# Token chunks of 512, 512 and 128 in place of three of 384 in the projections and the mixture of a hybrid encoder layer

## The chip, the core and the metric

The kernel runs on one core of a Trainium2 chip. The metric is the device time of one execution in microseconds (us). TensorE is called PE in the profile, its weight loads PEld; VectorE is DVE, ScalarE is ACT, GpSimd is POOL and SyncE is SP. A `q` behind a name (SPq) is the queue in which that engine issues its transfers.

## What is computed

One layer of a streaming encoder for 1024 prompt tokens (one sequence) and 128 sample tokens (8 sequences of 16), width 1024. What matters here is the first half of the layer:

```python
h = rmsnorm(x, norm1_g) * (1 + sc1) + sh1
q, k, v, cb, cc, cv, ga, gb = jnp.split(h @ w_in, IN_SPLITS, axis=-1)   # 6 x 512, then 2 x 1024 columns
att = prompt_attention(q, k, v, rel_bias)          # sample_attention for the sample tokens
u = cc * cv;  y = sum(conv_w[j] * u_pad[:, j:j + L] for j in range(3)) + conv_b;  conv_out = cb * y
mix = (jax.nn.sigmoid(ga) * (att @ w_pa) + jax.nn.sigmoid(gb) * (conv_out @ w_pb)) @ w_o
x = x + gt1 * mix
```

The second half is a router and a mixture of 32 experts, which the change doesn't touch.

## The kernel before

**Precision.** Every float32 product is made of three matmuls (`product`, lines 1562 to 1567). Weights and activations are split into a high part, rounded to the type fp32r by ACT, and a low part, the remainder, made by DVE; the three are high by high, high by low and low by high. In `chunk_of` and in the mixture the stationary operand of a matmul is a 128x128 tile of the weights (in `ring_r`), the moving operand is a run of token columns of the activations (`hTh`, `hTl`), and the result is a piece of a PSUM bank of 512 float32 columns.

**Tokens.** The 1152 tokens lie side by side, the 128 sample tokens last. They are cut in three chunks of 384 columns (`TOKCH`, line 41). The last chunk, columns 768 to 1151, holds 256 prompt tokens and the 128 sample tokens; where prompt and sample results go to different tiles, `parts` (line 69) cuts it in two, and its evacuation is two instructions.

**Projections.** A unit is a slice of 128 output columns of a weight matrix, a 128x1024 tile. `project` (line 1589) runs over 4 units and for each over the three chunks; a chunk of a unit is 8 products, 24 matmuls, into one of the banks 4 to 7 in turn. `group` makes PE wait, before it writes a bank, until the evacuation of the group four before it has been counted (`gev_qk`, `gev_conv`, `cu_done`). Five matrices go this way: Q, K, CC, CV and CB of the convolution. V and the output projection have the weights as the moving operand, 512 wide, and don't use the chunks. ACT evacuates Q, K and CC, DVE multiplies CV into it (line 1229), and CB into the convolution's result Y (line 1258). Between CV and CB, DVE computes the convolution itself, for all four tiles, before its first multiplication by CB.

**First unit.** The first two chunks of unit 0 of Q are computed inside the loop over the nine token tiles of the first norm, at its steps t = 7 and 8 (lines 1620 to 1624). Each waits until DVE has finished as many token tiles as it covers (`n1_lo`).

**Mixture.** 24 steps (line 1781): for each of the 8 output tiles f, the three chunks. A step is 24 products, 72 matmuls: gate A and gate B (8 products each) and the projections of attention and convolution (4 each), into four banks; the steps alternate between banks 0 to 3 and 4 to 7. ACT takes the two sigmoids, DVE two multiplications and the sum, POOL writes the result to DRAM (`mix_d`). PE may start step i when step i - 2 is done (`g_done`). The weights of tile f + 1 are brought in, and split by ACT and DVE, during step 0 of tile f.

**End of the mixture.** The last weights of the output projection need the ring's slots, and are issued by SP once all matmuls of the mixture are done (`g_ready`, line 426).

Of the kernel before, what the change touches and what calls it, by code (L numbers as in the profile page):

```python
# [5 lines left out]
ALU = mybir.AluOpType  # L6
# [7 lines left out]
P = 128  # L14
D = 1024
KT = D // P
NP_TOK, SEQS, DEC = 1024, 8, 16
NS_TOK = SEQS * DEC
T = NP_TOK + NS_TOK
# [17 lines left out]
OVF = (2 * T) // CAP - 1  # L37
NBLK = E + OVF
SEQROW = SEQS
TC = T // 3  # L40
TOKCH = [(0, TC), (TC, TC), (2 * TC, TC)]


class Link:
# [17 lines left out]
def wait(eng, sem, value):  # L62
# [1 line left out]
    if isinstance(value, int) and value <= 0:  # L64
        return
    eng.wait_ge(sem, value)


def parts(c0, cn):

    out = []
    if c0 < NP_TOK:
        out.append((c0, min(c0 + cn, NP_TOK) - c0, False))
    if c0 + cn > NP_TOK:
        start = max(c0, NP_TOK)
        out.append((start, c0 + cn - start, True))
    return out


def build(nc, x_prompt, x_sample, cache_attn_k, cache_attn_v, state_conv, c_prompt, c_sample,  # L80
# [4 lines left out]
    with ExitStack() as ctx:  # L85
# [4 lines left out]
        def at(name, shape, offset, dt=F32):  # L90
            return nc.alloc_sbuf_tensor_at(name, shape, dt, offset=base + int(offset))
# [68 lines left out]
        def A(kb):  # L160
            return ARENA + kb * KB
# [10 lines left out]
        kT = at("kT", [P, HP, NP_TOK], A(90))  # L172
        kTs = at("kTs", [P, HP, NS_TOK], A(106))
# [36 lines left out]
        U = at("U", [P, HP, NP_TOK + 2], A(90))  # L210
# [80 lines left out]

        ps = psum("ps", [P, 8, 512])

        def u_part(m, c0, t0, tn, sample, g):
            src = ps[:, 4 + g % 4, t0 - c0:t0 - c0 + tn]
            if sample:
                return Us[:, m, :, 2:], src.rearrange("p (q t) -> p q t", t=DEC)
            return U[:, m, 2 + t0:2 + t0 + tn], src

        def bank(b, n=1):  # L300
            return ps[:, b:b + n, :].rearrange("p b c -> p (b c)")
# [16 lines left out]
        s = {n: sem(n) for n in names}  # L318
# [15 lines left out]
        UQ, UK, UV, UCC, UCV, UCB = [4 * i for i in range(6)]  # L334
# [172 lines left out]
        def _(pool):  # L507
# [121 lines left out]
            for i in range(24):  # L629
                f, (c0, cn) = i // 3, TOKCH[i % 3]  # L630
                pool.wait_ge(s["g_done"], i + 1)
# [91 lines left out]
        def _(act):  # L723
# [56 lines left out]
            g = 0  # L780
            for what in range(2):
                for m in range(HP):
                    for c0, cn in TOKCH:
                        if c0 == 0:
                            weights_high_to(4 * what + m + 3)
                        act.wait_ge(s["gemm"], g + 1)
                        src = ps[:, 4 + g % 4, 0:cn]
                        if what == 0:
                            nc.scalar.mul(qT[:, m, c0:c0 + cn], src, HD ** -0.5).then_inc(s["gev_qk"], 1)
                        else:  # L790
                            for t0, tn, sample in parts(c0, cn):
                                dst = kTs[:, m, t0 - NP_TOK:t0 - NP_TOK + tn] if sample else kT[:, m, t0:t0 + tn]
                                nc.scalar.copy(dst, src[:, t0 - c0:t0 - c0 + tn]).then_inc(s["gev_qk"], 1)
                        g += 1
            weights_high_to(UV + 4)
            for i in range(5):
# [59 lines left out]
            for m in range(HP):  # L856
                weights_high_to(UCC + m + 2)
                for c0, cn in TOKCH:
                    act.wait_ge(s["gemm"], g + 1)
                    for t0, tn, sample in parts(c0, cn):  # L860
                        nc.scalar.copy(*u_part(m, c0, t0, tn, sample, g)).then_inc(s["gev_conv"], 1)
                    g += 1


# [4 lines left out]
                weights_high_to(UCV + m + 3)  # L869
            g += 12 + 2  # L870
            act.wait_ge(s["conv_last"], 1)
            act.wait_ge(s["cu_done"], 17)

            nc.scalar.copy(atth[:], qT[:]).then_inc(s["b_hi"], 1)
            for m in range(HP):
                act.wait_ge(s["gemm"], g + 3 * m + 1)
                weights_high_to(UCB + m + 3)
                act.wait_ge(s["cu_done"], 16 + 3 * (m + 1))
                nc.scalar.copy(Yh[:, m, :], Y[:, m, :]).then_inc(s["b_hi"], 1)

            def mixture_high(t):
# [6 lines left out]
            for i in range(24):  # L888
                cn = TOKCH[i % 3][1]
                if i % 3 == 0:  # L890
# [104 lines left out]
            with act.If(n_ov > 0):  # L995
                with act.Fori(0, OVF) as o:
                    with act.If(o < n_ov):
# [10 lines left out]
                        dst = y_d.rearrange("(p b) d -> p b d", b=NBLK)[:, bass.ds(o + E, 1), :]  # L1008
# [31 lines left out]
        def _(dve):  # L1040
            link = Link(dve, s["link_dve"])
            V = nc.vector
# [23 lines left out]
            n = P - 1 + BAND - 4 * P  # L1066
# [149 lines left out]
            g = 12 + 12 + 5 + NT  # L1216
# [5 lines left out]
            for m in range(HP):  # L1222
                weights_rest_to(UCV + m + 3)
                for n, (c0, cn) in enumerate(TOKCH):
                    dve.wait_ge(s["gemm"], g + 1)
                    for t0, tn, sample in parts(c0, cn):
                        dve.wait_ge(s["gev_conv"], 4 * m + n + 1 + sample)
                        dst, src = u_part(m, c0, t0, tn, sample, g)
                        V.tensor_tensor(dst, dst, src, ALU.mult).then_inc(s["cu_done"], 1)
                    g += 1  # L1230
            dve.wait_ge(s["cu_done"], 16)
            dve.wait_ge(s["gemm"], g + 1)
            V.tensor_copy(Us[:, :, :, 0:2],
                          ps[:, 4 + g % 4, 0:HP * 16].rearrange("p (m q j) -> p m q j", m=HP, j=2)
# [20 lines left out]
            for m in range(HP):  # L1255
                for c0, cn in TOKCH:
                    dve.wait_ge(s["gemm"], g + 1)
# [276 lines left out]
        def _(pe):  # L1534
# [3 lines left out]
            n = SEQS + 1  # L1538
# [47 lines left out]
                                   hTh[:, k, c0:c0 + cn], hTl[:, k, c0:c0 + cn], k == 0, k == KT - 1)  # L1586
                last.then_inc(s["gemm"], 1)

            def project(u0, owner, base_count, split=False):

                done = 0
                for m in range(4):
                    for c, (c0, cn) in enumerate(TOKCH):
                        done += len(parts(c0, cn)) if split else 1
                        if u0 > 0 or m > 0 or c == len(TOKCH) - 1:
                            chunk_of(u0 + m, c, owner, base_count + done)
                        if c0 == 0:
                            release(u0 + m - 1)
                    used[1] = len(owners)
# [16 lines left out]
            for t in range(NT):  # L1616
                r = t % 2
                if 1 <= t < NADA - LEAD:
                    modulation(LEAD + t)
                if t >= NT - 2:  # L1620
                    c = t - (NT - 2)
                    pe.wait_ge(s["mod_sb"], NADA)
                    pe.wait_ge(s["n1_lo"], (c + 1) * TC // P)
                    chunk_of(UQ, c, "gev_qk", c + 1)
                pe.wait_ge(s["n1_h"], t + 1)
                wait(pe, s["n1_lo"], t - 1)
                for k in range(KT):
                    last = tr(bank(2 * r, 2)[:, k * P:(k + 1) * P], ht[:, r, k * P:(k + 1) * P], ident[:])
                last.then_inc(s["n1_tr"], 1)
            pe.wait_ge(s["n1_lo"], NT)  # L1630
            pe.wait_ge(s["mod_sb"], NADA)

            project(UQ, "gev_qk", 0)
            project(UK, "gev_qk", 12, True)
            pe.wait_ge(s["gev_qk"], 28)
            for i in range(5):
                b = group("gev_kout", i + 1)
                for m in range(HP):
                    src = kT[:, m, (4 + i) * P:(5 + i) * P] if i < 4 else kTs[:, m, :]
# [123 lines left out]
            pe.wait_ge(s["ks_at"], H * SEQS)  # L1763


            project(UCC, "gev_conv", 0, True)
            project(UCV, "cu_done", 0, True)
            pe.wait_ge(s["prev_in"], 16)
            b = group("gev_prev", 1)
            for m in range(HP):  # L1770
# [4 lines left out]
            for m in range(HP):  # L1775
                last = tr(ps[0:18, b, m * P:(m + 1) * P], lastu[:, m, :], ident[:])
            last.then_inc(s["gemm"], 1)
            project(UCB, "cu_done", 16)


            for i in range(24):
                f, (c0, cn) = i // 3, TOKCH[i % 3]
                if i == 1:
                    pe.wait_ge(s["cu_done"], 28)
                ua, ub, up = [slot_of(UGATE + 3 * f + j) for j in range(3)]
                wait(pe, s["g_done"], i - 1)
                b = 4 * (i % 2)
                for kind, (sl, un, k0, kn, xh, xl, br) in enumerate((
                        (ua, 0, 0, KT, hTh, hTl, 0), (up, 2, 0, 4, atth, attl, 1),
                        (ub, 1, 0, KT, hTh, hTl, 0), (up, 2, 4, 4, Yh, Yl, HP + 1))):  # L1790
                    if i % 3 == 0:
                        pe.wait_ge(s["w_lo"], UGATE + 3 * f + un + 1)
                        wait(pe, s["b_lo"], br)
                    for k in range(kn):
                        last = product(ps[:, b + kind, 0:cn], ring_r[:, sl, 0, k0 + k, :],
                                       ring_r[:, sl, 1, k0 + k, :], xh[:, k, c0:c0 + cn], xl[:, k, c0:c0 + cn],
                                       k == 0, k == kn - 1)
                    last.then_inc(s["g_ready"], 1)
                    if i == 0 and kind == 0:
                        release(UCB + 3)  # L1800
                    if i == 23 and kind in (1, 3):
                        pe.wait_ge(s["g_ready"], 4 * i + kind)
                        pe.sem_inc(s["unit_used"], 1)
                    if i % 3 == 0 and f > 0 and kind == 0:
                        pe.wait_ge(s["g_ready"], 4 * i)
                        pe.sem_inc(s["unit_used"], 3)
# [194 lines left out]
```

## Time and profile before

| | us |
|---|---|
| median of 3 runs | 1923.19 (1922.13 to 1927.28) |
| span of the profiled execution, from first to last instruction | 1918.4 |
| PE busy (matmuls) | 1676.0 (87%), 8467 matmuls |
| PE busy (weight loads) | 1388.9 (72%) |
| DVE busy | 962.2 (50%) |
| ACT busy | 766.2 (40%) |

The profile gives no total of its own for the profiled execution beside its span, which is 4.8 us shorter than the median of the runs. Busy time is the union of the durations of an engine's instructions. Matmuls are pipelined: a matmul is shown with a duration that reaches past the start of the next one, so the cost of one in a dense stream is read from start to start and not from its duration.

The first projections run until about 260 us, with an idle stretch of PE before 169 us; V and attention fill 260 to 570, the projections of the convolution 570 to 730, the mixture 730 to 1030, the output projection and the second norm 1030 to 1180. After that come routing and the experts.

### The profile page before, as it was taken

How to read it: one execution, taken by the hardware profiler on the slowest of the kernel's cores; microseconds unless marked ns; L12 is line 12 of the kernel's file. 1: busy time of each engine (PE TensorE's matmuls, PEld its weight loads, DVE VectorE, ACT ScalarE, POOL GpSimd, SP SyncE). 2: the span in 40 equal slices, each digit the busy share in tenths (PEclk: the TensorE clock that was granted, in tenths of full speed). 3: DMA queues.
4: the chain of work that ended last, by engine and by line, in shares of the span. 5: the costliest groups of instructions: out<-in, count | busy, mean ns of one | idle time of the engine just before them, and what ended most of it. 6: DMA issues, size and time to landing. Idle time of an engine off the chain costs nothing.

```text
span 1918.4 us, 22477 instructions
## 1 busy us (share of the span) xinstructions
PE 1676.0 (87%) x8467; PEld 1388.9 (72%) x8467; DVE 962.2 (50%) x1156; ACT 766.2 (40%) x869; POOL 216.4 (11%) x336
## 2 busy tenths in 40 slices
PE   6984999999989989999998994499999999999930
PEld 1244987886449989999997883377777777777720
DVE  0451102554320272222223545488888888888847
ACT  0221123663112022111121322077777777777734
POOL 2004401110000000000000002100000000000036
PEclk9997999999999999999998997699999999999965
DMA  9857512003421111211225333299999999999963
GB/s 344 284 84 219 191 64 71 1 2 113 157 68 54 44 34 31 83 50 50 58 71 199 121 99 110 92 398 398 396 396 395 395 394 394 396 391 393 342 220 142
DMA packets 194747, 371.34 MB, mean 194 GB/s; under 512 B 10699, under 2 KB 69107, under 8 KB 194546
## 3 DMA queue, kind: packets, MB, share of 16 engines
q1 hardware_dynamic: 170784, 289.92, 42.1%
q0 software_dynamic: 18976, 62.93, 10.2%
q10 hardware_dynamic: 4914, 17.49, 2.3%
q8 instruction: 51, 0.84, 0.2%
q14 instruction: 22, 0.18, 0.0%
HBM read 324.49 MB, written 47.89 MB: 194 GB/s over the span
## 4 chain that ended last, share of the span: by engine, by line
PE 74%; DVE 10%; ACT 6%; issue 3%; DMA 2%; another core or an unknown queue 2%; ACTq 1%; POOL 0%; SPq 0%; POOLq 0%; DVEq 0%; PEldq 0%
PE ps L1565 19%; PE ps L1567 18%; PE ps L1566 18%; PE ps L1548 4%; DVE mlo L1084 4%; ACT mhi L938 3%; PE ps L1692 3%; PE ps L1673 2%; ACT yy L958 2%; PE ps L1755 2%; PE ps L1732 2%; PE ps L1879 2%; PE ps L1682 1%; DMA bada<-in_b_ada_dram 1%
## 5 line engine op out<-in xcount | busy, mean ns | idle before, releaser
L1084 DVE TENSOR_TENSOR mlo<-mraw,mhi 128x2048 fp32r<-128x2048 f32 x188 | 420.5, 2288 | 38.9 <-ACT mhi L938 38.7
L938 ACT CAST mhi<-mraw 128x2048 fp32r<-128x2048 f32 x192 | 357.2, 1910 | 27.3 <-DMA mraw<-in_w_e_down_dram 27.2
L1565 PE MATMUL ps<-hTh,ring_r 128*128 128x384 f32 x864 | 291.2, 337 | 39.5 <-DVE ring_r L1084 31.6
L1567 PE MATMUL ps<-hTh,ring_r 128*128 128x384 f32 x864 | 290.6, 336 | 0.0
L1566 PE MATMUL ps<-hTl,ring_r 128*128 128x384 f32 x864 | 290.6, 336 | 0.0
L1565 PE MATMUL ps<-mhi,xTh 128*128 128x512 f32 x512 | 207.5, 405 | 22.0 <-DVE mlo L1084 19.6
L1566 PE MATMUL ps<-mlo,xTh 128*128 128x512 f32 x512 | 201.7, 394 | 0.0
L1567 PE MATMUL ps<-mhi,xTl 128*128 128x512 f32 x512 | 201.5, 394 | 0.0
L1565 PEld LDWEIGHTS ps<-hTh,ring_r 128*128 128x128 f32 x864 | 163.8, 190 | 41.2 <-DVE ring_r L1084 29.8
L1084 DVE TENSOR_TENSOR ring_r<-ring_f,ring_r 128x1024 fp32r<-128x1024 f32 x56 | 68.2, 1224 | 199.9 <-ACT ring_r L748 199.5
L1567 PEld LDWEIGHTS ps<-hTh,ring_r 128*128 128x128 f32 x864 | 163.6, 189 | 0.0
L1566 PEld LDWEIGHTS ps<-hTl,ring_r 128*128 128x128 f32 x864 | 163.5, 189 | 0.0
L1565 PEld LDWEIGHTS ps<-mhi,xTh 128*128 128x128 f32 x512 | 97.3, 190 | 53.9 <-DVE mlo L1084 28.5
L1567 PEld LDWEIGHTS ps<-mhi,xTl 128*128 128x128 f32 x512 | 97.1, 190 | 21.1
L1566 PEld LDWEIGHTS ps<-mlo,xTh 128*128 128x128 f32 x512 | 97.3, 190 | 18.6
L1565 PE MATMUL ps<-mhi,hhTh 128*128 128x512 f32 x256 | 103.3, 404 | 6.3 <-DVE mlo L1084 6.3
L1567 PE MATMUL ps<-mhi,hhTl 128*128 128x512 f32 x256 | 100.9, 394 | 0.0
L1566 PE MATMUL ps<-mlo,hhTh 128*128 128x512 f32 x256 | 100.7, 393 | 0.0
L748 ACT CAST ring_r<-ring_f 128x1024 fp32r<-128x1024 f32 x56 | 58.5, 1051 | 105.1 <-DMA ring_f<-in_w_in_dram 45.9
L1548 PE MATMUL ps<-aring,cT 128*9 128x512 f32 x192 | 87.7, 611 | 8.0 <-DMA bada<-in_b_ada_dram 8.0
L943 ACT CAST xTh<-ps 128x1024 fp32r<-128x1024 f32 x32 | 32.5, 1016 | 114.9 <-PE ps L1879 114.9
L1130 DVE CUSTOM_DVE_ANT_0 S<-ps,bias 128x640 f32<-128x640 f32 (+4 forms) x64 | 42.1, 657 | 63.3 <-PE ps L1674 63.2
(302 smaller groups left out, 2549.4 us busy)
## 6 DMA issues: line engine op xcount, KB each, us to landing
mraw<-in_w_e_gate_dram SPq DMA_DIRECT2D x64, 1024.0 KB
mraw<-in_w_e_up_dram SPq DMA_DIRECT2D x64, 1024.0 KB
mraw<-in_w_e_down_dram SPq DMA_DIRECT2D x64, 1024.0 KB, 7.9
aring<-in_w_ada_dram SPq DMA_DIRECT2D x24, 1024.0 KB
ring_f<-in_w_in_dram SPq DMA_DIRECT2D x80, 256.0 KB, 4.5
y_d<-yy ACTq DMA_DIRECT2D x32, 512.0 KB, 6.8
y_d<-zrow POOLq DMA_DIRECT2D x68, 128.0 KB, 4.0
kc<-in_cache_attn_k_dram SPq DMA_DIRECT2D x8, 1024.0 KB, 5.3
```

What stands on the lines that cost most here:

```text
L748: nc.scalar.copy(ring_r[:, sl, 0], ring_f[:, sl, 1]).then_inc(s["w_hi"], 1)
L938: nc.scalar.copy(mhi[j][:], mraw[j][:]).then_inc(s["gu_hi" if j < 4 else "d_hi"], 1)
L958: nc.scalar.copy(yy[:, r, :], bank(5, 2)).then_inc(s["y_ok"], 1)
L1084: V.tensor_tensor(out, value, high.bitcast(F32), ALU.subtract).then_inc(sig, 1)
L1130: link(V.tensor_tensor_reduce(out=S[:, a % 2, c0:BAND], in0=bank(2 * (a % 2), 2)[:, c0:BAND], in1=bias[:, h, c0:BAND], scale=1.0, scalar=- ...
L1548: last = mm(ps[0:n, 4 + u % 2, :], cT[:, k, :], aring[u % 4][:, k, :], start=(k == 0), stop=(k == KT - 1))
L1565: mm(out, xh, wh, start=start, stop=False)
L1566: mm(out, xh, wl, start=False, stop=False)
L1567: return mm(out, xl, wh, start=False, stop=stop)
L1673: mm(bank(2 * (a % 2))[:, j0 * P:512], q, kT[:, hp, k0:i * P], start=True, stop=True)
L1692: last = mm(ps[:, 6, HD * h_:HD * h_ + HD], PT[:, a % 2, j, :], v[:, i - 4 + j, (2 * hp + h_) * HD:(2 * hp + h_ + 1) * HD], start=(j == j0 ...
L1732: mm(ps[:, 4, :], qb[:, m, :], kcT[:, m, :], start=(m == 0), stop=(m == HP - 1))
```

## The change

The chunks become columns 0 to 511, 512 to 1023 and 1024 to 1151. The last chunk is now exactly the sample tokens, so that `parts` goes away, each evacuation is one instruction, and the counts of the semaphores shrink from 4 to 3 per unit for K, CC and CV. The number of matmuls and weight loads and the total of columns stay the same. In the norm's loop the first chunk waits for 4 token tiles in place of 3, the second for 8 in place of 6.

```diff
-TC = T // 3
-TOKCH = [(0, TC), (TC, TC), (2 * TC, TC)]
+TOKCH = [(0, 512), (512, 512), (NP_TOK, NS_TOK)]
-def parts(c0, cn):
...
-        def u_part(m, c0, t0, tn, sample, g):
-            src = ps[:, 4 + g % 4, t0 - c0:t0 - c0 + tn]
-            if sample:
+        def u_part(m, c0, cn, g):
+            src = ps[:, 4 + g % 4, 0:cn]
+            if c0 == NP_TOK:
                 return Us[:, m, :, 2:], src.rearrange("p (q t) -> p q t", t=DEC)
-            return U[:, m, 2 + t0:2 + t0 + tn], src
+            return U[:, m, 2 + c0:2 + c0 + cn], src
...
-                            for t0, tn, sample in parts(c0, cn):
-                                dst = kTs[:, m, t0 - NP_TOK:t0 - NP_TOK + tn] if sample else kT[:, m, t0:t0 + tn]
-                                nc.scalar.copy(dst, src[:, t0 - c0:t0 - c0 + tn]).then_inc(s["gev_qk"], 1)
+                            dst = kTs[:, m, :] if c0 == NP_TOK else kT[:, m, c0:c0 + cn]
+                            nc.scalar.copy(dst, src).then_inc(s["gev_qk"], 1)
...
-                    for t0, tn, sample in parts(c0, cn):
-                        dve.wait_ge(s["gev_conv"], 4 * m + n + 1 + sample)
-                        dst, src = u_part(m, c0, t0, tn, sample, g)
-                        V.tensor_tensor(dst, dst, src, ALU.mult).then_inc(s["cu_done"], 1)
+                    dve.wait_ge(s["gev_conv"], 3 * m + n + 1)
+                    dst, src = u_part(m, c0, cn, g)
+                    V.tensor_tensor(dst, dst, src, ALU.mult).then_inc(s["cu_done"], 1)
...
-                    pe.wait_ge(s["n1_lo"], (c + 1) * TC // P)
+                    pe.wait_ge(s["n1_lo"], 4 * (c + 1))
```

## Rows read from the trace of the kernel before

**Rows 1.** The page, chain of work that ended last: shares of the span.
```profile
PE 74%; DVE 10%; ACT 6%; issue 3%; DMA 2%; another core or an unknown queue 2%; ACTq 1%; POOL 0%; SPq 0%; POOLq 0%; DVEq 0%; PEldq 0%
```
**Rows 2.** Groups by line and form: line, operation, shapes, count, busy us, mean ns, idle.
```profile
L1565 PE MATMUL ps<-hTh,ring_r 128*128 128x384 f32 x864 | 291.2, 337 | 39.5 <-DVE ring_r L1084 31.6 <-DVE Y L1258 3.9 <-DVE hTl L1097 2.4
...
L1565 PE MATMUL ps<-atth,ring_r 128*128 128x384 f32 x96 | 32.2, 335 | 0.2 <-DVE ring_r L1084 0.2
...
L1565 PE MATMUL ps<-Yh,ring_r 128*128 128x384 f32 x96 | 32.1, 334 | 0.0
```
**Rows 3.** Stretches: us, busy us (count) of PE, PEld, DVE, ACT, POOL; granted clock; DMA.
```profile
355.00:455.00 100.00, 99.45 (x723) 84.62 (x721) 55.71 (x204) 61.09 (x136) 12.06 (x40) 1.00 0.01 1
674.00:730.00 56.00, 52.08 (x290) 51.44 (x289) 36.06 (x44) 11.43 (x8) 1.04 (x2) 0.97 0.13 39
730.00:1030.00 300.00, 299.72 (x1728) 299.08 (x1726) 73.38 (x99) 53.39 (x77) 17.32 (x23) 1.00 0.20 58
1217.00:1222.00 5.00, 4.02 (x18) 3.90 (x18) 3.27 (x6) 0.00 (x0) 0.00 (x0) 0.50 0.00 0
```
**Rows 4.** Order of time, PE, one chunk (start us, duration us): matmuls 2 and 24.
```profile
122.49 0.33 PE L1566 MATMUL ps<-hTl,ring_r 128*128 128x384 f32 x1
...
126.30 0.34 PE L1567 MATMUL ps<-hTh,ring_r 128*128 128x384 f32 x1
```
**Rows 5.** Order of time, PE, output projection: two matmuls, twelve starts apart.
```profile
1065.95 0.39 PE L1565 MATMUL ps<-ring_r,mixh 128*128 128x512 f32 x1
...
1068.67 0.39 PE L1565 MATMUL ps<-ring_r,mixh 128*128 128x512 f32 x1
```
**Rows 6.** Order of time, PE and PEld: narrow operations; the first four in attention.
```profile
400.39 0.71 PE L1682 MATMUL ps<-ident,Pr 128*128 128x128 f32 x5
400.94 1.00 PE L1692 MATMUL ps<-v,PT 128*128 128x64 f32 x8
...
400.83 0.97 PEld L1692 LDWEIGHTS ps<-v,PT 128*128 128x128 f32 x8
401.72 0.30 PEld L1673 LDWEIGHTS ps<-kT,qz 128*128 128x128 f32 x2
...
1217.65 2.12 PE L1870 MATMUL ps<-oneblk,onerow 128*128 128x50 f32 x9 [30.11 <-DVE oneblk L1430]
```
**Rows 7.** Order of time, PE and ACT: the restart of PE at unit 1.
```profile
168.84 0.69 PE L1565 MATMUL ps<-hTh,ring_r 128*128 128x384 f32 x1 [29.46 <-DVE ring_r L1084]
...
166.48 1.04 ACT L748 CAST ring_r<-ring_f 128x1024 fp32r<-128x1024 f32 x1 [32.85 <-DMA ring_f<-in_w_in_dram]
```
**Rows 8.** Order of time, PE and DVE: the start of CB, groups 5 and 6.
```profile
693.69 0.44 PE L1565 MATMUL ps<-hTh,ring_r 128*128 128x384 f32 x1 [3.16 <-DVE Y L1258]
...
700.49 0.45 PE L1565 MATMUL ps<-hTh,ring_r 128*128 128x384 f32 x1 [0.76 <-DVE Y L1258]
...
693.08 0.55 DVE L1258 TENSOR_TENSOR Y<-Y,ps 128x384 f32<-128x384 f32 x1
...
699.88 1.01 DVE L1258 TENSOR_TENSOR Y<-Y,ps 128x384 f32<-128x384 f32 x2
```
**Rows 9.** Order of time, ACT and DVE: last evacuations of K and of CV.
```profile
257.86 0.37 ACT L793 COPY kT<-ps 128x256 f32<-128x256 f32 x1 [3.69 <-PE ps L1567]
258.13 0.27 ACT L793 COPY kTs<-ps 128x128 f32<-128x128 f32 x1
...
672.02 0.42 DVE L1229 TENSOR_TENSOR U<-U,ps 128x256 f32<-128x256 f32 x1 [3.61 <-PE ps L1567]
672.36 0.28 DVE L1229 TENSOR_TENSOR Us<-Us,ps 128x128 f32<-128x128 f32 x1
```
**Rows 10.** Mixture: a group of ACT by form, and a transfer's issue to landing.
```profile
L897 ACT ACTIVATE sgA<-ps 128x384 f32<-128x384 f32 x24 | 11.8, 492 | 130.8 <-PE ps L1567 130.8
...
mix_d<-mixc POOLq DMA_DIRECT2D x1, 192.0 KB, 4.5
```
**Rows 11.** Chain that ended last, in order of time, behind the mixture.
```profile
1032.66 8.09 DMA ring_f<-in_w_o_dram
```

More of the change, by code:

```diff
@@ L66, in wait @@
     eng.wait_ge(sem, value)
-def parts(c0, cn):
[L71 to L77, printed above, removed]
 def build(nc, x_prompt, x_sample, cache_attn_k, cache_attn_v, state_conv, c_prompt, c_sample,
@@ L859, in _ @@
                     act.wait_ge(s["gemm"], g + 1)
-                    for t0, tn, sample in parts(c0, cn):
-                        nc.scalar.copy(*u_part(m, c0, t0, tn, sample, g)).then_inc(s["gev_conv"], 1)
+                    nc.scalar.copy(*u_part(m, c0, cn, g)).then_inc(s["gev_conv"], 1)
                     g += 1
@@ L871, in _ @@
             act.wait_ge(s["conv_last"], 1)
-            act.wait_ge(s["cu_done"], 17)
+            act.wait_ge(s["cu_done"], 13)
             nc.scalar.copy(atth[:], qT[:]).then_inc(s["b_hi"], 1)
@@ L877, in _ @@
                 weights_high_to(UCB + m + 3)
-                act.wait_ge(s["cu_done"], 16 + 3 * (m + 1))
+                act.wait_ge(s["cu_done"], 12 + 3 * (m + 1))
                 nc.scalar.copy(Yh[:, m, :], Y[:, m, :]).then_inc(s["b_hi"], 1)
@@ L1225, in _ @@
                     dve.wait_ge(s["gemm"], g + 1)
-                    for t0, tn, sample in parts(c0, cn):
-                        dve.wait_ge(s["gev_conv"], 4 * m + n + 1 + sample)
-                        dst, src = u_part(m, c0, t0, tn, sample, g)
-                        V.tensor_tensor(dst, dst, src, ALU.mult).then_inc(s["cu_done"], 1)
+                    dve.wait_ge(s["gev_conv"], 3 * m + n + 1)
+                    dst, src = u_part(m, c0, cn, g)
+                    V.tensor_tensor(dst, dst, src, ALU.mult).then_inc(s["cu_done"], 1)
                     g += 1
-            dve.wait_ge(s["cu_done"], 16)
+            dve.wait_ge(s["cu_done"], 12)
             dve.wait_ge(s["gemm"], g + 1)
@@ L1587, in chunk_of, with project @@
                 last.then_inc(s["gemm"], 1)
-            def project(u0, owner, base_count, split=False):
+            def project(u0, owner, base_count):
                 done = 0
@@ L1593, in project @@
                     for c, (c0, cn) in enumerate(TOKCH):
-                        done += len(parts(c0, cn)) if split else 1
+                        done += 1
                         if u0 > 0 or m > 0 or c == len(TOKCH) - 1:
@@ L1633, in _ @@
             project(UQ, "gev_qk", 0)
-            project(UK, "gev_qk", 12, True)
-            pe.wait_ge(s["gev_qk"], 28)
+            project(UK, "gev_qk", 12)
+            pe.wait_ge(s["gev_qk"], 24)
             for i in range(5):
@@ L1763, in _ @@
             pe.wait_ge(s["ks_at"], H * SEQS)
-            project(UCC, "gev_conv", 0, True)
-            project(UCV, "cu_done", 0, True)
+            project(UCC, "gev_conv", 0)
+            project(UCV, "cu_done", 0)
             pe.wait_ge(s["prev_in"], 16)
@@ L1777, in _ @@
             last.then_inc(s["gemm"], 1)
-            project(UCB, "cu_done", 16)
+            project(UCB, "cu_done", 12)
             for i in range(24):
@@ L1783, in _ @@
                 if i == 1:
-                    pe.wait_ge(s["cu_done"], 28)
+                    pe.wait_ge(s["cu_done"], 24)
                 ua, ub, up = [slot_of(UGATE + 3 * f + j) for j in range(3)]
```

## The prediction, made before the changed kernel was run

> **What bounds the kernel now.** I read the shares of the chain first, then the groups by form, then the stretches, and last the starts of single matmuls. PE carries 74% of the chain [rows 1]. The matmuls that the change touches are 864 + 96 + 96 on each of three lines, 3168 in all, all 384 wide [rows 2], where lines 1566 and 1567 have the same counts. In the mixture PE is busy for 299.72 of 300 us, at the full clock, with DVE at 73 and ACT at 53 us [rows 3]. So in these stages the time is the number of matmuls by their distance from start to start, and the evacuations lie beside it. The question of the case is what a matmul of 128 columns costs, since the total of columns stays and only their cut changes.
>
> **The distance of wide matmuls.** In a chunk of 384, 22 matmuls start between 122.49 and 126.30, 173.2 ns each [rows 4]. At 512 wide, 12 start in 2.72 us, 226.7 ns each [rows 5]. So 128 columns more cost 53.5 ns, and the columns alone would put a matmul of 128 at 173.2 - 2 x 53.5 = 66.2 ns. By that line the new cut costs nothing: 2 x 226.7 + 66.2 = 3 x 173.2 = 519.6 ns.
>
> **The distance of a narrow one.** The rows say that the line ends before 128 columns. Five transposes of 128 columns take the 0.55 us from 400.39 to 400.94, 110 ns each; eight weight loads behind matmuls of only 64 columns take 400.83 to 401.72, 111 ns each [rows 6]. Half the columns, the same distance: what they share is a load of a full 128x128 float32 tile, one for each matmul. Those are plain float32. The one narrow fp32r form of the trace is the routing's (50 columns, `onerow` and `oneblk`): nine matmuls in 2.12 us, less a duration of about 0.39, 8 steps of 216 ns [rows 6], at half clock (1.2 GHz) [rows 3]. The column line gives 66.2 - 78 x 0.418 = 33.6 ns there, 67 at half clock; measured is three times that, and half of 216 is 108. So the loads of fp32r tiles set the same floor, and a matmul of 128 columns will stand at 108 to 120 ns. The lower end is the floor by itself. The upper adds the part of the wide matmuls that isn't columns, 173.2 - 3 x 53.5 = 12.7 ns, in case it comes on top of a load. I take 112, next to the rows of 110 and 111.
> The Trainium skill has a rule that speaks for the change: TensorE: Matmul & The Clock Gate, section Back-to-back issue gap, gives about 56 ns for an isolated gap at 128 columns, and says that weight loads raise it to about 81 ns in a real stream. By 81 the three would be 534.4 ns, 14.8 more than now, some 15 us in all (an estimate from that page). The same page's section LDWEIGHTS gives 128 columns / 1.2 = 107 ns for a load, and with that the trace agrees (110 and 111 ns).
>
> **The main term.** Three matmuls at one weight position become 2 x 226.7 + 112 = 565.4 ns, 45.8 more. There are 3168 / 3 = 1056 such threes. The 24 of unit 0 of Q lie ahead of the wait of 29.46 us that ends at 168.84 [rows 7]. It ends with the split of unit 1, whose ACT cast had itself waited 32.85 us for its DMA; that DMA doesn't depend on the chunks. The three longer chunks and the new wait of the second chunk for token tile 8 (a few us: a transpose, an ACT copy, a DVE subtraction) fit in these 29 us, and cost nothing; without that cover they would cost some 1 + 4 us. Left are 1032 x 45.8 ns = 47.3 us.
>
> **CB.** PE runs four groups ahead of the convolution on DVE, then waits 3.16 us for the first multiplication, and once more before 700.49 for the second [rows 8]. Both waits end with DVE, which the change hardly moves: the first two multiplications grow by about 0.14 us each (0.55 for 384 columns, 0.42 for 256 [rows 8, 9]). The first four groups become 24 x (3 x 226.7 + 112) = 19.0 us in place of 16.6 and hide in the wait. So the sixth group starts at about 700.6 again. Behind it stand seven groups, 7 x 4.16 = 29.1 us before; after, one of 2.7 and two units of 13.6, 29.8 us. CB costs 0.8 us, where the main term counts 96 x 45.8 = 4.4. That gives back 3.6 us. The stretch also has a reduced clock now (0.97 [rows 3]); a shorter first wait can only help.
>
> **Edges.** The last evacuation of K, two copies one after the other from 257.86, becomes one of 0.27, about 0.3 us earlier; that of CV, 0.42 + 0.28 on DVE, becomes 0.28, about 0.4 us earlier [rows 9]. PE waits for both. They give back 0.7 us.
>
> **Mixture.** A step of 512 takes 72 x 226.7 = 16.3 us, the narrow one 72 x 112 = 8.1. PE may start step i when step i - 2 is evacuated, so the cover of the middle step falls from 12.5 to 8.1 us. Behind the last matmul of a step come a sigmoid of about 0.6 us, a multiplication and a sum of about 0.7 each (0.49 and 0.55 at 384 now), 2 us in all: covered. The sum of the narrow step waits for the transfer of the one before, 4.5 us at 192 KB [rows 10], perhaps 6 at 256: about as long as the narrow step, and what waits behind it is needed only 16 us later. ACT idles 130.8 us before 24 sigmoids, 5.4 each [rows 10]; the split of the next tile's weights lies in step 0, which gets longer. Nothing here. Behind the mixture the chain runs through the transfers of the last weights, issued when the last matmul is done (8.09 us [rows 11]); they move with it. The last steps release two slots some 1 to 3 us later against that end, which I bound at 0 to 1 us and take as 0.
>
> **Sum.** 47.3 - 3.6 - 0.7 = +43.0 us. The profiled span is 1918.4, 4.8 below the median of the runs; the whole change lies inside the span, so I add it to the median: 1923.2 + 43.0 = 1966.2. With 108 ns the main term is 1032 x 41.8 = 43.1, less 3.3 and 0.7: +39. With 120 ns it is 55.5, less 4.3 and 0.7: +50.5. Changes of the granted clock after short waits add about 2 us on either side, so this case alone gives 1960 to 1976.
>
> **Rivals.**
> **(B) The columns decide, not the load.** If fp32r loads hide behind the matmul before them down to 66 ns, the main term is zero, and CB still gains: its last seven groups take 1.6 + 2 x 12.5 = 26.6 us in place of 29.1. With the edges that is 3.2 us less, 1920.0, not slower. It decides for any distance below 66.2 + 3 = 69 ns. For it speaks that wide matmuls show no sign of their loads; against it speak 110 and 111 ns, and 216 at half clock. By the page's 56 ns this is the outcome; by its 81 ns it would be some 11 to 15 us slower.
> **(C) fp32r is fast only when it is wide.** A matmul of 128 columns costs as much as one of 512, 226.7 ns. Then each three costs 160.5 more, 1032 x 160.5 = 165.6 us, less what CB hides: about 2085. The 50 columns don't exclude it: four times 50 columns at half clock would be 4 x 50 x 0.836 = 167 ns, below the measured 216.
> **(D) The narrow steps lower the clock.** In attention, in the stretch 355 to 455 us, matmuls of 64 and 128 columns run at clock 1.00 [rows 3], though mixed with wide ones. If the narrow steps of the mixture ran at half clock, their 576 matmuls would cost some 100 ns more each, +58 us: about 2024. The narrow chunks of the projections, 2.7 us each between wide ones, are less exposed.
>
> **Chances.** The forecast 0.82, B 0.06, C 0.05, D 0.04, a distance between 70 and 105 ns 0.03 (about 1935). Range 1958 to 1979: the forecast's case with a small margin on each side, which leaves out the rest. About 0.3%, 6 us, can be told from no change. Faster than that: 0.01. Within it: 0.06 (B). Slower: 0.93.
>
> **What would show it.** Starts in a narrow chunk 108 to 120 ns apart, in a wide one 226 to 227. The mixture's stretch 300 + 192 x 3 x 45.8 ns = about 326 us, still full. Unit 1 of Q at 168.8 as before, with some 24 to 26 us of idle time ahead of it. The first wait of CB below 1 us, and CB's end at about the same distance from its start. Granted clock 1.00 in the mixture. Wrong it would be made by a distance of the narrow ones outside 108 to 120, by waits of PE for ACT or DVE inside the mixture, or by a lower clock there.

## The result, and the profile after

| | before | after |
|---|---|---|
| median of the runs, us | 1924.38 (1922.13 to 1927.28) | 1962.78 (1961.69 to 1965.34) |
| span of the profiled execution, us | 1918.4 | 1961.7 |
| PE busy (matmuls), us | 1676.0 | 1725.4 |
| PE busy (weight loads), us | 1388.9 | 1353.2 |

The ratio of the runs is 1.0214, with a 95% interval of 1.02 to 1.0228. Of 1924.38 us that is 41.2 us (38.5 to 43.9). The two medians of the table alone lie 38.4 us apart, the two profiled spans 43.3 us. In the nine executions that have both a time and a profile, the span is 1.6 to 1.8 us below the time. So the profiled execution of the kernel before took about 1920.1 us (an estimate), less than any of its four timed runs, and the spans lie further apart than the medians.

The groups of PE by line and form (line, operation, shapes, count, busy us, mean ns, idle) answer to [rows 2]. Line 1550 of the new kernel is line 1565 of the old one:
```profile
L1550 PE MATMUL ps<-hTh,ring_r 128*128 128x512 f32 x576 | 227.9, 396 | 30.7 <-DVE ring_r L1070 25.7 <-DVE hTl L1083 2.5 <-DVE qT L1173 1.7
...
L1550 PE MATMUL ps<-hTh,ring_r 128*128 128x128 f32 x288 | 78.7, 273 | 3.6 <-DVE hTl L1083 2.4 <-DVE Y L1243 1.2
```
The 864 matmuls of the line are now 576 wide and 288 narrow. A narrow step of the mixture in order of time (start us, duration us), its first two matmuls and the 24th, answers to [rows 4]:
```profile
822.16 0.22 PE L1550 MATMUL ps<-hTh,ring_r 128*128 128x128 f32 x1
822.21 0.28 PE L1551 MATMUL ps<-hTl,ring_r 128*128 128x128 f32 x1
...
824.67 0.28 PE L1552 MATMUL ps<-hTh,ring_r 128*128 128x128 f32 x1
```
From 822.21 to 824.67 there are 22 steps of 112 ns. The very first step is only 50 ns, and the first wide matmul behind the narrow ones is 0.30 us from its successor in place of 0.227 (830.14 to 830.44), so that the two edges of a narrow step nearly cancel. Why the first step is so short isn't shown.

The mixture as a stretch (us; busy us and count of PE, PEld, DVE, ACT, POOL; granted clock; DMA) answers to [rows 3]:
```profile
748.80:1074.80 326.00, 325.95 (x1729) 280.45 (x1727) 72.67 (x99) 52.97 (x77) 16.01 (x23) 1.00 0.19 54
```
It is as full as before and at the same clock, only longer: from its first to its last matmul 325.8 us in place of 299.65. No wait for ACT or DVE came in.

The milestones of PE tell where the rest is. Of the kernel before, the first matmuls of V, of CC, the transposes between CV and CB, and the first matmul on `atth`, one gate A after the start of the mixture:
```profile
261.79 0.50 PE L1565 MATMUL ps<-ring_r,hTh 128*128 128x512 f32 x1 [0.30 <-DVE ring_r L1084]
...
570.30 0.44 PE L1565 MATMUL ps<-hTh,ring_r 128*128 128x384 f32 x1 [1.69 <-DVE qT L1187]
...
673.27 0.39 PE L1776 MATMUL ps<-ident,lastu 128*18 128x128 f32 x2 [0.94 <-DVE lastu L1238]
...
734.27 0.44 PE L1565 MATMUL ps<-atth,ring_r 128*128 128x384 f32 x1 [0.20 <-DVE ring_r L1084]
```
The same of the kernel after, with its restart at unit 1 ahead and the two waits inside CB:
```profile
170.76 0.80 PE L1550 MATMUL ps<-hTh,ring_r 128*128 128x512 f32 x1 [23.58 <-DVE ring_r L1070]
...
271.35 0.50 PE L1550 MATMUL ps<-ring_r,hTh 128*128 128x512 f32 x1 [0.31 <-DVE ring_r L1070]
...
579.41 0.50 PE L1550 MATMUL ps<-hTh,ring_r 128*128 128x512 f32 x1 [1.69 <-DVE qT L1173]
...
691.22 0.39 PE L1761 MATMUL ps<-ident,lastu 128*18 128x128 f32 x2 [0.70 <-DVE lastu L1223]
...
711.79 0.50 PE L1550 MATMUL ps<-hTh,ring_r 128*128 128x512 f32 x1 [0.89 <-DVE Y L1243]
...
718.74 0.33 PE L1550 MATMUL ps<-hTh,ring_r 128*128 128x128 f32 x1 [1.21 <-DVE Y L1243]
...
754.22 0.39 PE L1550 MATMUL ps<-atth,ring_r 128*128 128x512 f32 x1
```

| stage | before, us | after, us | difference | predicted |
|---|---|---|---|---|
| start to the restart at unit 1 [rows 7] | 168.84 | 170.76 | +1.9 | 0 |
| 7 units of Q and K | 92.95 | 100.59 | +7.6 | +7.4 |
| V and attention | 308.5 | 308.1 | -0.4 | 0 |
| CC and CV | 102.97 | 111.81 | +8.8 | +8.4 |
| CB (without the first gate A: 4.16, then 5.44 us) | 56.84 | 57.56 | +0.7 | +0.8 |
| mixture | 299.65 | 325.81 | +26.2 | +26.4 |
| its end to the second half of the first output tile | 13.4 | 14.3 | +0.9 | 0 (bounds 0 to 1) |
| the rest | 875.3 | 872.8 | -2.5 | 0 |

The sum is 43.2, to rounding the distance of the two spans.

The first line isn't the change's. The first chunk of unit 0 begins later too, by 2.06 us, and nothing that the change touches lies before it (before, then after):
```profile
122.24 0.41 PE L1565 MATMUL ps<-hTh,ring_r 128*128 128x384 f32 x1 [2.10 <-DVE ring_r L1084]
...
124.30 0.47 PE L1550 MATMUL ps<-hTh,ring_r 128*128 128x512 f32 x1 [2.10 <-DVE ring_r L1070]
```
In all ten profiled executions this first chunk begins somewhere between 120.5 and 124.7 us, and the restart follows it by 46.3 to 47.3 us, whatever the cut.

In the last line, 1.3 of the 2.5 us lie before the first transposes of the second norm (1165.74 before, 1210.16 after). The output projection there begins at the reduced clock of 1.2 GHz, and stays at it for some 6 us before and some 3 us after:
```profile
1043.20:1049.20 6.00, 6.00 (x15) 4.70 (x16) 1.15 (x1) 0.00 (x0) 0.00 (x0) 0.51 1.03 409
...
1092.20:1098.00 5.80, 5.80 (x27) 4.79 (x26) 1.82 (x2) 0.00 (x0) 0.00 (x0) 1.00 0.74 265
```
Some 3 us less at half clock are worth about 1.6 us (an estimate). The remaining 1.2 us weren't followed.

### The profile page after: what moved, and what is told of

It reads as the page before. It is cut to its first block, busy times and chain, and to the rows that moved or that the text cites. A ratio compares the mean times of both kernels' runs of the same rounds, so it can differ in the third digit from the quotient of the medians.

```text
span 1961.7 us, 22465 instructions
## 1 busy us (share of the span) xinstructions
PE 1725.4 (88%) x8467; PEld 1353.2 (69%) x8467; DVE 961.4 (49%) x1152; ACT 766.0 (39%) x861; POOL 217.5 (11%) x336
## 4 chain that ended last, share of the span: by engine, by line
PE 75%; DVE 10%; ACT 6%; issue 3%; DMA 2%; another core or an unknown queue 1%; ACTq 1%; POOL 0%; SPq 0%; POOLq 0%; DVEq 0%; PEldq 0%
PE ps L1550 19%; PE ps L1552 18%; PE ps L1551 18%; PE ps L1533 4%; DVE mlo L1070 4%; ACT mhi L924 3%; PE ps L1677 3%; PE ps L1658 2%; ACT yy L944 2%; PE ps L1740 2%; PE ps L1717 1%; PE ps L1864 1%; PE ps L1667 1%; DMA bada<-in_b_ada_dram 1%
## 5 line engine op out<-in xcount | busy, mean ns | idle before, releaser
L1550 PE MATMUL ps<-hTh,ring_r 128*128 128x512 f32 (+1 forms) x864 | 306.6, 355 | 34.3 <-DVE ring_r L1070 25.7
L1552 PE MATMUL ps<-hTh,ring_r 128*128 128x512 f32 (+1 forms) x864 | 306.1, 354 | 0.0
L1551 PE MATMUL ps<-hTl,ring_r 128*128 128x512 f32 (+1 forms) x864 | 305.4, 353 | 0.0
L1272 DVE TENSOR_TENSOR sgA<-sgA,ps 128x512 f32<-128x512 f32 (+1 forms) x24 | 13.3, 555 | 130.3 <-PE ps L1552 130.3
```

The lines of the kernel that those rows point to most:

```text
L1550: mm(out, xh, wh, start=start, stop=False)
L1551: mm(out, xh, wl, start=False, stop=False)
L1552: return mm(out, xl, wh, start=False, stop=stop)
```

## The experiments

In what follows, theory L is that a narrow matmul waits for the load of its own 128x128 float32 tile. Rival S is that a narrow fp32r matmul streams its columns more slowly. Both give 112 ns at 128 columns, so the two sides of the tile were changed one at a time. Beside the first four experiments the kernel before took 1920.2 us, beside the last four 1921.0 (medians).

### Half the moving columns

The narrow chunk moves 64 columns, and half of the sample tokens' results are stale.
```diff
-                    last = product(ps[:, b, 0:cn], ..., hTh[:, k, c0:c0 + cn], hTl[:, k, c0:c0 + cn], ...)
+                    mv = cn if cn > P else P // 2
+                    last = product(ps[:, b, 0:mv], ..., hTh[:, k, c0:c0 + mv], hTl[:, k, c0:c0 + mv], ...)
```
The same stands in the mixture.

> The changed kernel, but the narrow chunk of the projections and the mixture moves only the first 64 of the 128 sample tokens through the array; the other 64 columns of each bank are left at what an earlier group wrote. Number of matmuls and weight loads unchanged. Theory L (a narrow matmul waits for the load of its 128x128 float32 tile): starts in the narrow chunk stay 111 ns apart, and the time stays that of the changed kernel, 1962 to 1964 us. Rival S (a narrow fp32r matmul streams its columns at a lower rate, 111 ns for 128): 64 columns take about 56 ns, 1032 x 55 ns = 57 us less, about 1906. If columns at the wide rate decided (39 ns) it would be lower still.

Measured: 2010.8 us, ratio 1.0468 (1.045 to 1.0486). Neither theory had foreseen a slower kernel. The trace splits the total in two. A narrow chunk of the projections, second and last matmul:
```profile
685.63 0.27 PE L1551 MATMUL ps<-hTl,ring_r 128*128 128x64 f32 x1
...
688.09 0.28 PE L1552 MATMUL ps<-hTh,ring_r 128*128 128x64 f32 x1
```
22 steps in 2.46 us are 112 ns: half the columns, the same distance. S (56 ns) falls, and L's number holds. But the mixture looks like this, as stretches: the whole, one piece around a narrow step, and the piece behind it:
```profile
750.00:1121.00 371.00, 370.99 (x1730) 322.54 (x1729) 72.67 (x99) 52.59 (x77) 15.97 (x23) 0.87 0.17 48
...
786.80:797.00 10.20, 10.20 (x44) 9.62 (x44) 0.87 (x3) 0.28 (x1) 0.55 (x1) 0.50 0.04 14
797.10:831.20 34.10, 34.10 (x166) 28.71 (x164) 7.63 (x9) 5.50 (x8) 1.50 (x2) 1.00 0.19 54
```
PE never rests, yet the clock falls to 1.2 GHz in the course of each of the eight narrow steps, and the wide step behind it begins there too. The matmuls of such a piece stand twice as far apart:
```profile
790.00 0.40 PE L1551 MATMUL ps<-hTl,ring_r 128*128 128x64 f32 x1
...
794.06 0.40 PE L1552 MATMUL ps<-Yh,ring_r 128*128 128x64 f32 x1
```
19 steps in 4.06 us, 214 ns. The stretch is 45 us longer than the changed kernel's 326, most of the 49 us by which this kernel stands above it. That is the mechanism of rival D, here with 64 columns. With 128 columns, and otherwise the same instructions, the clock is 1.00.

The clock fell once more, in the projections: inside a narrow chunk of CB which began behind a wait of 1.22 us for DVE.
```profile
716.92 0.30 PE L1550 MATMUL ps<-hTh,ring_r 128*128 128x64 f32 x1 [1.22 <-DVE Y L1243]
...
718.60:725.00 6.40, 6.40 (x21) 5.46 (x21) 6.40 (x6) 1.10 (x2) 0.00 (x0) 0.50 0.05 16
```

### Half the stationary columns

The narrow chunk loads 64 of the 128 weight columns, and half of the rows of its results are stale.
```diff
-                    last = product(ps[:, b, 0:cn], ring_r[:, sl, 0, k, :], ring_r[:, sl, 1, k, :], ...)
+                    st = P if cn > P else P // 2
+                    last = product(ps[0:st, b, 0:cn], ring_r[:, sl, 0, k, 0:st], ring_r[:, sl, 1, k, 0:st], ...)
```
The same stands in the mixture.

> The changed kernel, but in the narrow chunk each matmul loads only 64 of the 128 weight columns (64 of the 128 rows of the result are left at what an earlier group wrote); all 128 sample tokens still move. Theory L: the load takes half, about 56 ns, so the columns decide, 66 ns by the line through 384 and 512; 1032 x 45 ns = 46 us less than the changed kernel, less what the wait ahead of CB gives back twice (3 us): 1916 to 1922. Rival S (the rate of streaming is what is slow): the distance stays 111 ns, the time 1963.

Measured: 1912.5 us, ratio 0.9961 (0.9947 to 0.9975). Two matmuls of a narrow chunk, ten starts apart:
```profile
645.37 0.22 PE L1551 MATMUL ps<-hTl,ring_r 128*64 128x128 f32 x1
...
645.97 0.22 PE L1552 MATMUL ps<-hTh,ring_r 128*64 128x128 f32 x1
```
60 ns. The same 128 columns move almost twice as fast once the load is half as large, and the cost of the change is gone with it. A fixed price of 112 ns per matmul, whatever it loads or moves, falls too: the number of matmuls and loads is the same. The kernel even undercuts the one before by 7.5 us (4.8 to 10.2). For that, 60 ns in place of the 66 of the line through 384 and 512 account for 1032 x 6.2 ns = 6.4 us; what rival B gave to CB and the edges, 3.2 us, stands beside it within the interval. The expected band was worked out with 66 ns, which is why the total lies 3.5 us below it.

### Twice the moving columns

The 128 tokens are moved twice into 256 columns of the bank; the second half is not read.
```diff
+                    def cols_of(x):
+                        x = x[:, k, c0:c0 + cn]
+                        return x if cn > P else x.unsqueeze(1).to_broadcast([P, 2, P])
+                    mv = cn if cn > P else 2 * P
-                    last = product(ps[:, b, 0:cn], ..., hTh[:, k, c0:c0 + cn], hTl[:, k, c0:c0 + cn], ...)
+                    last = product(ps[:, b, 0:mv], ..., cols_of(hTh), cols_of(hTl), ...)
```
The same stands in the mixture.

> The changed kernel, but the narrow chunk moves its 128 tokens twice, into columns 0 to 127 and 128 to 255 of the bank; only the first 128 are read. Theory L: 256 columns are just wider than the load, the line through 384 and 512 gives 119.7 ns, so twice the columns cost 9 ns per matmul, 1032 x 9 = 9 us: 1970 to 1973. Rival S: 222 ns, 1032 x 111 = 115 us more, about 2078.

Measured: 1973.05 us, ratio 1.0277 (1.026 to 1.0294), at the upper edge of L's band (1970 to 1973) and 105 us below S. Second and last matmul of a narrow chunk:
```profile
607.87 0.28 PE L1551 MATMUL ps<-hTl,ring_r 128*128 128x256 f32 x1
...
610.50 0.28 PE L1552 MATMUL ps<-hTh,ring_r 128*128 128x256 f32 x1
```
22 steps in 2.63 us, 119.5 ns. The second 128 columns cost 8 ns. In the changed kernel every narrow matmul pays for about twice the columns that it moves.

### An uneven cut without a narrow chunk

The kernel before, with another cut; `parts` stays, and the first unit waits for as many token tiles as its chunks cover.
```diff
-TOKCH = [(0, TC), (TC, TC), (2 * TC, TC)]
+TOKCH = [(0, 512), (512, 384), (896, 256)]
```

> The kernel before, with chunks of 512, 384 and 256 columns. Theory L: 226.7 + 173.2 + 119.7 = 519.6 ns, the same as three of 384; behind the wait ahead of CB 128 columns more are done, 24 x 53 ns = 1.3 us less, the last chunk's evacuations a little shorter: 1920 to 1924. Rival U (an uneven cut costs by itself, through banks, evacuations or waits): slower, with waits of PE for ACT or DVE in the mixture.

Measured: 1922.2 us, ratio 1.0012 (1.0002 to 1.0021), +2.3 us (0.4 to 4.0), inside the expected band. The mixture of this kernel:
```profile
739.70:1034.30 294.60, 294.56 (x1705) 272.70 (x1703) 68.36 (x95) 49.55 (x74) 17.07 (x23) 1.00 0.20 57
```
This is the stretch without its first gate A (5.4 us, the first chunk is 512 wide): together 300 us, as with three of 384, and PE waits neither for ACT nor for DVE in it. So wide and unequal chunks cost at most some 4 us in all, of the change's 41; what costs is the one chunk whose matmuls stand further apart than its columns ask for. Rival U falls as an explanation of the change. The 1.3 us hoped for in CB don't show in the total.

### The mixture alone, the projections alone

```diff
 TOKCH = [(0, TC), (TC, TC), (2 * TC, TC)]
+MIXCH = [(0, 512), (512, 512), (1024, 128)]
...
-                f, (c0, cn) = i // 3, TOKCH[i % 3]
+                f, (c0, cn) = i // 3, MIXCH[i % 3]
```
The second kernel is the changed one with three of 384 in `MIXCH`.

> The kernel before, with the new cut in the mixture alone; the projections keep three chunks of 384. 576 threes by 2 x 226.7 + 111 - 519.6 = 44.8 ns are 25.8 us; the changed kernel's mixture took 326.0 us against 299.8. With up to 1 us more behind it (later release of two slots): +26 to +27 us, about 1947 beside a kernel before of 1920.2. If the 43 us of the whole change came in good part from elsewhere (restart, transfers, clock), this would be well below 26.

> The changed kernel, with three chunks of 384 in the mixture: the new cut in the projections alone. 360 threes of Q (three units), K, CC and CV by 44.8 ns are 16.1 us, CB 0.8, edges -0.7: +16 us. If the waits ahead of CB gave nothing back it would be +20. Together with the kernel that has the mixture alone it should add up to the whole change.

Measured: 1948.5 us for the mixture alone, ratio 1.0147 (1.013 to 1.0164), +28.2 us (25.0 to 31.5). 1938.2 us for the projections alone, ratio 1.0094 (1.0077 to 1.0111), +18.1 us (14.8 to 21.3). Both hold their numbers within their intervals. That of the projections holds both the 16 and the 20 us, so that it doesn't decide what the waits ahead of CB gave back; the next experiment is for that. The sum of the centres, 46, is above the 41.2 of the whole change, but well within what the intervals allow. A part of their scatter is the moment of the restart, which moved by some 4 us between executions with no order in the cuts:
```profile
170.67 0.69 PE L1567 MATMUL ps<-hTh,ring_r 128*128 128x384 f32 x1 [27.61 <-DVE ring_r L1086]
```
This is the mixture alone, whose chunks there are still 384 wide, and
```profile
166.96 0.80 PE L1552 MATMUL ps<-hTh,ring_r 128*128 128x512 f32 x1 [20.47 <-DVE ring_r L1072]
```
the projections alone, with the new chunks there. This agrees with what was said of the first line of the table.

### CB alone

```diff
+CBCH = [(0, 512), (512, 512), (1024, 128)]
...
-                for c0, cn in TOKCH:
+                for c0, cn in CBCH:
                     dve.wait_ge(s["gemm"], g + 1)
                     V.tensor_tensor(Y[:, m, c0:c0 + cn], ...
...
-            project(UCB, "cu_done", 16)
+            project(UCB, "cu_done", 16, cuts=CBCH)
```

> The kernel before, with the new cut in CB alone (PE's chunks of CB and DVE's multiplications by it). 96 threes by 44.8 ns would be 4.3 us; if the two waits for DVE's convolution take 3.5 of them back, the time grows by 0.8 us, which can't be told from none, and PE's end of CB comes 0.8 us later after its start than before. If they don't, it grows by 4 us (0.2%).

Measured: 1922.4 us, ratio 1.0007 (0.9997 to 1.0017). Start and end of the stage, the latter again one gate A of 4.16 us into the mixture:
```profile
675.05 0.61 PE L1777 MATMUL ps<-ident,lastu 128*18 128x128 f32 x4 [0.93 <-DVE lastu L1239]
...
736.75 0.44 PE L1566 MATMUL ps<-atth,ring_r 128*128 128x384 f32 x1
```
61.70 us against 61.00, +0.7 where the count of matmuls alone says +4.3. PE's waits for DVE's product Y in this stage are 2.0 us; before they were 3.9 [rows 2]. The trace shows the hidden part; the total, +1.4 us (-0.6 to +3.3), agrees with it and leaves little room for the 4 us of no hiding.

### Half the moving columns, in the projections alone

The first experiment's edit in `chunk_of` only; half of the sample tokens' results of the projections are stale.
```diff
-                    last = product(ps[:, b, 0:cn], ..., hTh[:, k, c0:c0 + cn], hTl[:, k, c0:c0 + cn], ...)
+                    mv = cn if cn > P else P // 2
+                    last = product(ps[:, b, 0:mv], ..., hTh[:, k, c0:c0 + mv], hTl[:, k, c0:c0 + mv], ...)
```

> The changed kernel, with 64 of the 128 columns moved in the narrow chunk of the projections alone; the mixture moves all 128. In the run with both halved, the narrow matmuls kept 112 ns at full clock, but the clock fell to half around each narrow step of the mixture. If it is these steps of 8 us that pull the clock down, and narrow chunks of 2.7 us between wide ones don't, the time is that of the changed kernel, +40 to +44 us over the kernel before, with clock 1.00 in the projections. If any narrow run of 64 columns does it, it is 10 us or more above. If the rate of streaming were the limit (rival S), 456 x 55 = 25 us below.

Measured: 1967.3 us (1960.0 to 1968.9), ratio 1.0248 (1.0231 to 1.0265), +47.6 us (44.4 to 50.9). That is some 4 us above the first of the two expectations, and below the second. CC with CV, the start of CB, CB, and the mixture as stretches:
```profile
578.00:688.00 110.00, 109.31 (x581) 93.95 (x582) 16.74 (x24) 13.79 (x20) 0.51 (x1) 1.00 0.19 53
689.00:692.20 3.20, 3.20 (x9) 2.49 (x8) 3.06 (x6) 0.00 (x0) 1.04 (x2) 0.50 0.13 29
690.00:745.00 55.00, 54.17 (x281) 46.09 (x281) 34.95 (x41) 11.43 (x8) 0.59 (x2) 0.98 0.14 40
745.00:1071.00 326.00, 326.00 (x1731) 280.68 (x1731) 72.53 (x99) 52.55 (x77) 15.97 (x23) 1.00 0.19 54
```
The clock is full in CC, CV and the mixture, and these stages are as long as in the changed kernel. A narrow chunk of 2.7 us that stood between wide ones without a wait never lowered the clock here, even with 64 columns; the 8 us steps of the first experiment did. But the clock fell where such a chunk met a wait: here behind the last chunk of CV and the short waits ahead of CB (0.50 from before 689.00 until after 692.20), in the first experiment inside a chunk of CB behind 1.22 us of waiting. In the changed kernel, with 128 columns, both places run at 1.00. The wait has a part in it, since the kernel before, whose chunks are all wide, also has a reduced clock in CB (0.97 [rows 3]); what the 64 columns add there isn't separated. S would have been 25 us faster and falls once more.

The profiled execution, with a span of 1958.2 us, was the fastest of the four by 7 us, and no stage of it is longer than in the changed kernel. The other three, spans 1965.3 to 1967.1 us, ran at a mean clock of 0.944 to 0.945 against its 0.947. That is some 9 to 13 us more at half clock, worth 4 to 6 us (an estimate). So the extra 4 us may be clock. That isn't shown, since these runs left no trace, and neither is the stage.

## Why the prediction was right

**The size.** Forecast were +43.0 us and 1966.2 us. Measured are 1962.8 us and +41.2 us by the ratio, whose interval holds the 43.0, and 43.3 us between the profiled spans. The medians alone say +38.4. The 4.8 us that the forecast took for the distance of span and median were mostly the scatter of executions (1.6 to 1.8 us elsewhere), which left the difference as it was.

**The narrow matmul.** The whole forecast hung on one number that the trace of before had in no row: an fp32r matmul of 128 columns. It was put at 112 ns between 108 and 120, from rows of plain float32 and from one fp32r form at half clock, against the line through the wide ones, which said 66. Measured are 112; that it was 112 and not 109 or 115 is in part luck, since the rows gave 108 to 111 and a few ns were laid on top. The reason given, the load of a full tile, was only argued then. It is shown now from both sides: half the moving columns leave 112, half the stationary ones give 60, twice the moving ones 119.5. Rivals B (66) and C (226.7) fall by the same rows. The narrow distances of attention were the right neighbours because they share the stationary tile, not because they share the width.
The figure of 81 ns from the Trainium skill's page TensorE: Matmul & The Clock Gate, section Back-to-back issue gap, and its isolated 56 ns, don't hold for these fp32r matmuls, which stand 112 ns apart; the measurement decides. Its section LDWEIGHTS (107 ns for 128 columns) came nearest.

**The main term** was +47.3 us over 1032 threes. By stages it came to 7.6 + 8.8 + 26.2 us, against 7.4, 8.4 and 26.4 predicted, edges included. Of the edges, the wait behind CV fell from 0.94 to 0.70 us, and the one behind K from 0.63 to 0.35:
```profile
258.45 1.97 PE L1640 MATMUL ps<-ident,kT 128*128 128x128 f32 x16 [0.63 <-ACT kTs L793]
...
268.01 1.97 PE L1625 MATMUL ps<-ident,kT 128*128 128x128 f32 x16 [0.35 <-ACT kTs L780]
```
Together that is 0.5 us of the 0.7 predicted.

**CB** was to hide 3.6 of its 4.4 us, and its +0.7 us says that it did: the first wait fell from 3.16 to 0.89 us ("below 1 us"), the second grew from 0.76 to 1.21.

**Hidden and free.** The first unit fitted in front of the restart: the idle time there went from 29.46 to 23.58 us, and the kernel with the mixture alone restarts at 170.67 without any of that work. The prediction had 24 to 26 us of it left. From the start of the first chunk to the idle stretch PE took 17.1 us before and 22.9 after, so that the new parts cost 5.7 us where it gave them 5. The narrower cover in the mixture was enough: PE never waited there.

**Too small to count.** Behind the mixture +0.9 us, at the top of the bound of 0 to 1, was taken as 0. The chain there:
```profile
1076.93 1.85 SPq L422
1078.82 7.69 DMA ring_f<-in_w_o_dram
```
The transfer itself is no longer than before [rows 11], but SP's issues ahead of it end later against the last matmul: 1078.82 is 4.2 us after 1074.6, where 1032.66 was 2.9 after 1029.76. Why the last issue took 1.85 us isn't shown.

**Rival D** didn't come true: the mixture ran at clock 1.00. But the argument against it, that attention runs narrow matmuls at full clock, didn't carry: with 64 moving columns the mixture's steps brought exactly this, for 45 us. Nothing was run between 64 and 128 columns, so the runs don't say how safe the changed kernel was from it. That the small chance was borne out is in this part luck.

## What to carry to other kernels

In these dense fp32r streams a matmul took the larger of two times, that of the columns it moves (226.7, 173.2 and 119.5 ns for 512, 384 and 256) and that of the load of its stationary tile (112 ns for 128x128); a chunk so narrow that the load wins pays for columns it doesn't move. When the number of matmuls is fixed, cut the moving side so that every chunk stays above that point: here 256 columns were enough, and 512, 384 and 256 cost the same as three of 384 to within 4 us of 1920. A price that no row has is best read from the rows that share the suspected limit, not from the line through the rows that share the shape.

## What was not expected of the hardware

TensorE's granted clock fell to half while it was never idle: in the mixture with 64 moving columns, 112 ns apart, PE was busy for 370.99 of 371 us, and yet each tile had a stretch at clock 0.50 like the 10.2 us shown, with 0.87 as the mean. The same matmuls in runs of 2.7 us between wide ones ran at clock 1.00 in CC and CV; where such a run met a wait of about 1 us, at the start of CB and inside it, the clock fell to 0.50 in or behind it. A full clock on a PE that is always busy can't be taken for granted when its matmuls are narrow; it has to be read for the stage itself.

A narrow matmul with a load of 64 columns stands 60 ns from the next, less than the 66 that the line through 384 and 512 columns gives. If its columns set the 60 ns, then of the 12.7 ns that a wide matmul takes beyond its columns (173.2 - 3 x 53.5) about half is gone with the smaller load (60 - 53.5 = 6.5). What that part is, and whether at 60 ns the columns or the half load (56 ns, half of 112) decide, wasn't tried.
